# Half expert blocks summed by a product with a unit matrix, down weights split on VectorE alone, block columns fetched three blocks ahead

## The chip, the core and the metric

The kernel runs on one core of a Trainium2 chip, as one launch. The metric is the device time in microseconds (us). A core has TensorE (PE, with its weight loads PEld), VectorE (DVE), ScalarE (ACT), GpSimd (POOL) and SyncE (SP); SBUF is the on-chip memory, and PSUM, in eight banks of 2 KB per partition, takes TensorE's results. GpSimd doesn't reach PSUM.

## What is computed

Two transformer layers follow each other on 256 tokens of 1024 features in fp32. The first has three kinds of attention with a gated merge; the second has a mixer (short convolution and an attention over selected keys) and a mixture of experts. The change touches the last alone:

```
scores = sigmoid(t @ w_router); eidx = top 8 of scores + bias        # 64 experts, 256 tokens
g = scores at eidx, normalised, times 2.5
for each expert e, in blocks of its tokens xb:
    routed[tokens] += ((silu(xb @ w1[e]) * (xb @ w3[e])) @ w2[e]) * g
x = x + gate2 * (routed + shared expert)
```

w1[e] and w3[e] are 1024 x 256, w2[e] is 256 x 1024, all fp32. TensorE multiplies in a faster fp32 form that rounds its inputs, so each operand is split into a rounded high part and the rest (low part), and products of high by high, high by low and low by high are added up.

## The kernel before

Everything ahead of the experts (some 650 us) follows a written-out schedule and isn't touched. Then the router's choice is turned into a list of blocks, `work`: the pieces of experts' token lists, large ones (up to 128 tokens) in even places and small ones (up to 64) in odd places. With these inputs 33 blocks are run, numbered i = 0 to 32; `r = i % 4` picks buffers. An even block I call **whole**, an odd one **half**, an even and the next odd one a pair. All engines run loops over the blocks, in an order written by hand, and meet only by semaphores.

- SyncE loads, three transfers of 1 MB per block, w1 and w3 (`load_up`, L748, once the low parts of the block two before are made) and w2 (`load_down`, L755), then a column of 8 numbers per token for block i + 2 (`load_columns`, L741). `load_down` of an even block waits for GpSimd too, by the semaphore `pool_lo`.
- ScalarE makes the high parts: `up_hi` (four pieces, L1191) and `down_hi` (two, L1196) of the weights, and those of the turned rows (L1180, L1186), of the hidden values (`round_hidden`, L1202) and of the results (L1211).
- VectorE makes the low parts, a subtraction of the raw tile and the high part each: `up_lo` (L1736), `down_lo` (L1743), `x_block_lo` (L1730, in half blocks' rows L1723), `h_lo` (L1782; L1800 in half blocks), `y_lo` (L1750). `take_tokens` (L1716 to L1718) reads out which tokens block i + 2 has.
- GpSimd: in half blocks one piece of `up_lo` of the next block (`rest_of_up_weights`, L940), in whole blocks one piece of `down_lo` (`rest_of_down_weights`, L933). For both kinds: `pick` (`make_pick`, two L914) for block i + 3 out of its columns, `put` (`make_put`, L947), the matrix that scatters block i's results and that waits for the scatter of the block before, and the gather of block i + 2's rows from HBM (`gather_rows`, L925). In half blocks `put` comes before the gather, in whole blocks behind it.
- TensorE per block (`expert_block`): which tokens (`find_tokens`, L2158), up products into the bank `hidden_b` (L2206: 24 in a whole block, 16 in a half block), turning of the next block's gathered rows (`turn_rows`, L2168 for 64 rows, L2175 for 128), scatter of the last block's results (L2183, eight), two turns of the hidden values into `turned_b` (L2226), down products (L2245: 12 or 8).

In a half block, high and low part of the up to 64 rows lie side by side as the 128 columns of one stationary operand. The upper and lower half of `hidden_b` are therefore two parts of one sum. ScalarE copies the lower half (L1249), VectorE adds the upper (L1793), ScalarE takes silu (L1252), VectorE multiplies (L1797), TensorE turns the product (L2226), ScalarE rounds it (L1202), VectorE takes the rest (L1800):

```
act.activation(hsum[0:HALF, :], hidden_b[HALF:P, :], ACT.Copy)              # L1249
dve.tensor_tensor(hsum[0:HALF, :], hidden_b[0:HALF, :], hsum[0:HALF, :], ALU.add)   # L1793
act.activation(hs[0:HALF, 0, :], hsum[0:HALF, 0:ED], ACT.Silu)              # L1252
dve.tensor_tensor(he[0:HALF], hs[0:HALF, 0, :], hsum[0:HALF, ED:2 * ED], ALU.mult)  # L1797
```

## Time and profile before

| what | value |
|---|---|
| median of 3 runs (lowest, highest) | 1045.25 us (1044.28, 1047.04) |
| the profiled execution, its time and its span | 1048.44 us, 1046.6 us |
| mean granted clock of TensorE | 0.984 |
| TensorE, VectorE, ScalarE, GpSimd busy | 971.1, 755.3, 584.4, 408.4 us |
| the same as shares of the span | 93%, 72%, 56%, 39% |
| moved by DMA, mean rate | 238.55 MB, 228 GB/s |

Times in the trace count from the start of the span; its time is 1.84 us longer than its span. L numbers are lines of the kernel before. A row such as "675.78 0.77 PE L2245 ... [6.67 <-POOL down_lo L933]" says: start, length, engine, line, and that the engine had stood for 6.67 us, ended by GpSimd's write of `down_lo` at L933. The length of a TensorE record holds its way through the array; how fast products follow each other is read from their starts. "issue" in a chain is time in which the engine waited for nothing that the profile shows.

### The profile page before, as it was taken

How to read it: one execution, taken by the hardware profiler on the slowest of the kernel's cores; microseconds unless marked ns; L12 is line 12 of the kernel's file. 1: busy time of each engine (PE TensorE's matmuls, PEld its weight loads, DVE VectorE, ACT ScalarE, POOL GpSimd, SP SyncE). 2: the span in 40 equal slices, each digit the busy share in tenths (PEclk: the TensorE clock that was granted, in tenths of full speed). 3: DMA queues.
4: the chain of work that ended last, by engine and by line, in shares of the span. 5: the costliest groups of instructions: out<-in, count | busy, mean ns of one | idle time of the engine just before them, and what ended most of it. 6: DMA issues, size and time to landing. Idle time of an engine off the chain costs nothing. (4 is left out here: it accounts for less than half of the span.)

```text
span 1046.6 us, 16235 instructions
## 1 busy us (share of the span) xinstructions
PE 971.1 (93%) x4988; PEld 771.8 (74%) x4988; DVE 755.3 (72%) x1319; ACT 584.4 (56%) x896; POOL 408.4 (39%) x392
## 2 busy tenths in 40 slices
PE   8999999999999899999969999699899999999996
PEld 7778877778776676777758877477677777777774
DVE  4677888769753453556795554588898888888987
ACT  4555655444433432435433531487787887787875
POOL 5154453124100000041234411456666657666564
PEclk9999999999999899999998999899999999999998
DMA  9877677668635234425423223878888888888883
GB/s 312 280 258 264 222 240 274 224 203 283 228 101 181 96 101 181 161 82 183 143 99 137 86 88 141 292 275 330 311 304 328 339 303 338 310 303 338 316 327 134
DMA packets 79286, 238.55 MB, mean 228 GB/s; under 512 B 12732, under 2 KB 18933, under 8 KB 65922
## 3 DMA queue, kind: packets, MB, share of 16 engines
q1 hardware_dynamic: 66002, 196.60, 52.2%
q0 software_dynamic: 12656, 40.87, 11.5%
q8 instruction: 29, 0.48, 0.2%
q10 hardware_dynamic: 576, 0.41, 0.1%
q14 instruction: 23, 0.19, 0.1%
HBM read 235.55 MB, written 2.16 MB: 227 GB/s over the span
## 5 line engine op out<-in xcount | busy, mean ns | idle before, releaser
L1925 PE MATMUL bank<-w_hi,a_hi 128*128 128x512 f32 (+2 forms) x512 | 206.0, 402 | 10.0 <-DVE w_lo L1341 4.5
L1925 PE MATMUL bank<-w_hi,a_lo 128*128 128x512 f32 (+2 forms) x512 | 196.8, 384 | 0.0
L1925 PE MATMUL bank<-w_lo,a_hi 128*128 128x512 f32 (+2 forms) x512 | 196.5, 384 | 0.0
L1341 DVE TENSOR_TENSOR w_lo<-ring,w_hi 128x1024 fp32r<-128x1024 f32 (+2 forms) x132 | 152.8, 1181 | 52.6 <-ACT w_hi L1026 48.6
L1026 ACT ACTIVATE w_hi<-ring 128x1024 fp32r<-128x1024 f32 (+2 forms) x140 | 141.0, 1023 | 73.9 <-PE bank L1925 70.2
L1736 DVE TENSOR_TENSOR up_lo<-raw_weights,up_hi 128x1024 fp32r<-128x1024 f32 x120 | 144.4, 1239 | 2.9 <-ACT up_hi L1191 2.0
L1191 ACT ACTIVATE up_hi<-raw_weights 128x1024 fp32r<-128x1024 f32 x136 | 135.8, 1051 | 2.2 <-DMA raw_weights<-in_w_dram 2.2
L1925 PEld LDWEIGHTS bank<-w_hi,a_hi 128*128 128x128 f32 x512 | 96.5, 188 | 39.7 <-issue 18.0
L811 POOL TENSOR_SCALAR mean_squares<-mean_squares 128x8 f32<-128x8 f32 (+2 forms) x32 | 10.4, 324 | 283.6 <-ACT logits L979 203.5
L1925 PEld LDWEIGHTS bank<-w_hi,a_lo 128*128 128x128 f32 x512 | 96.5, 188 | 20.0
L1925 PEld LDWEIGHTS bank<-w_lo,a_hi 128*128 128x128 f32 x512 | 96.7, 189 | 18.3 <-issue 1.4
L2206 PE MATMUL bank<-up_hi,x_block_hi 128*128 128x512 f32 x264 | 107.2, 406 | 0.7 <-DVE x_block_lo L1730 0.7
L2206 PE MATMUL bank<-up_lo,x_block_hi 128*128 128x512 f32 x264 | 104.2, 395 | 0.0
L831 POOL DMA_DIRECT2D merged<-in_w_ada_dram x96 | 53.2, 556 | 127.2 <-DVE ada_acc L1480 93.9
L2245 PE MATMUL bank<-down_hi,h_hi 128*128 128x512 f32 x132 | 54.8, 415 | 24.1 <-DVE h_hi L1800 14.9
L914 POOL TENSOR_SCALAR pick<-slots,block_cols 128x128 fp32r<-128x128 f32 x72 | 51.2, 721 | 62.1 <-DMA block_cols<-pcol 60.6
L1196 ACT ACTIVATE down_hi<-raw_weights 128x1024 fp32r<-128x1024 f32 x68 | 69.8, 1055 | 0.2
L940 POOL TENSOR_TENSOR up_lo<-raw_weights,up_hi 128x1024 fp32r<-128x1024 f32 x16 | 43.9, 2741 | 63.2 <-ACT up_hi L1191 63.2
L1480 DVE SCALAR_TENSOR_TENSOR ada_acc<-merged,c_col,ada_acc 128x512 f32<-128x512 f32 x84 | 62.8, 747 | 5.1 <-DMA merged<-in_w_ada_dram 2.0
L947 POOL TENSOR_SCALAR put<-slots,block_tokens_f 128x256 fp32r<-128x256 f32 x33 | 59.7, 1810 | 14.8 <-PE bank L2183 14.8
L1743 DVE TENSOR_TENSOR down_lo<-raw_weights,down_hi 128x1024 fp32r<-128x1024 f32 x50 | 59.6, 1219 | 0.2 <-ACT down_hi L1196 0.2
L925 POOL DMA_INDIRECT x_gathered<-h_rows,block_tokens x35 | 51.4, 1469 | 20.8 <-issue 14.7
(283 smaller groups left out, 1968.4 us busy)
## 6 DMA issues: line engine op xcount, KB each, us to landing
raw_weights<-in_w_dram SPq DMA_DIRECT2D x102, 1024.0 KB, 6.9
ring<-in_w_in_dram SPq DMA_DIRECT2D x58, 1024.0 KB, 6.0
merged<-in_w_ada_dram POOLq DMA_DIRECT2D x96, 256.0 KB, 4.3
ring<-in_w_out_dram SPq DMA_DIRECT2D x8, 1024.0 KB, 6.0
ring<-in_w_branch_dram SPq DMA_DIRECT2D x6, 1024.0 KB, 4.9
bias<-rel_rows SPq DMA_DIRECT2D x40, 128.0 KB, 5.1
ring<-in_ws_dram SPq DMA_DIRECT2D x2, 1024.0 KB, 5.5
merged<-in_x_dram SPq DMA_DIRECT2D x2, 512.0 KB, 5.1
```

What stands on the lines that cost most here:

```text
L831: gp.dma_start(ada_row(q), src).then_inc(S(f"ada_loaded_{q % ADA_SLOTS}"), 16)
L947: gp.tensor_scalar(put[:, :], slots[:, S_TOK:S_TOK + TOK], tok_f[:, r, 0:1], None, ALU.is_equal)\
L1026: act.activation(w_parts[0][:, 2 * p:2 * p + 2, 0:w], view(j, kind)[:, 2 * p:2 * p + 2, :], ACT.Copy)\
L1191: act.activation(up_hi[:, r % 2, 4 * kh:4 * kh + 4, m, :], raw_up(raw[:, 1 - r % 2, :], kh, m), ACT.Copy)\
L1196: act.activation(down_hi[:, f, :], raw[:, 1 - r % 2][:, UP + f * DM:UP + (f + 1) * DM], ACT.Copy)\
L1341: dve.tensor_tensor(w_parts[1][:, 2 * p:2 * p + 2, 0:w], view(JOB[it[1:3]], kind)[:, 2 * p:2 * p + 2, :], w_parts[0][:, 2 * p:2 * p + 2, 0 ...
L1480: dve.scalar_tensor_tensor(out=o, in0=ada_row(q), scalar=c_col[:, 1, k:k + 1], in1=o, op0=ALU.mult, op1=ALU.add) .then_inc(S("ada_step" if ...
L1736: dve.tensor_tensor(up_lo[:, r % 2, 4 * kh:4 * kh + 4, m, :], raw_up(raw[:, 1 - r % 2, :], kh, m), up_hi[:, r % 2, 4 * kh:4 * kh + 4, m, : ...
L1743: dve.tensor_tensor(down_lo[:, f, :], raw[:, 1 - r % 2][:, UP + f * DM:UP + (f + 1) * DM], down_hi[:, f, :].bitcast(F32), ALU.subtract).th ...
L1925: mm = pe.matmul(ps[:, 0:wide], a_parts[za][:, k, t * P:(t + 1) * P], w_parts[zw][:, k, 0:wide], start=start, stop=stop)
L2206: mm = pe.matmul(hidden_b[:, :], (xe_hi, xe_lo)[zx][:, k, :], (up_hi, up_lo)[zw][:, r % 2, k].rearrange("p m n -> p (m n)"), start=(k == 0 ...
L2245: mm = pe.matmul(y_b[hf][:, :], (h_hi, h_lo)[zh][:, f, :], (down_hi, down_lo)[zw][:, f, hf * CH:hf * CH + CH], start=(n == 0), stop=(n == ...
```

## The change

Three things, all in the expert loop.

1. In half blocks ScalarE copies the whole of `hidden_b` to `halves`. Four products with `S_PAIR`, 64 columns that have a one at row j and at row j + 64, add the two halves and turn them at once into `turned_b`. TensorE waits for them (for `tokens_ready` too, since the found tokens lie in the same bank), ahead of the scatter. Silu, product and both parts are then taken in the turned form; the two turns of L2226 go in half blocks.
2. GpSimd's `rest_of_down_weights` goes; VectorE makes both pieces of `down_lo` in whole blocks. The waits on `pool_lo` shrink to those for `up_lo`, and SyncE's `load_down` waits for VectorE alone.
3. Columns are loaded three blocks ahead, two blocks' columns at the start.

The order of instructions on three engines moves with it. TensorE in a half block, from the turning of the next rows to the down products, before:

```order
L2175 MATMUL bank<-consts,x_gathered 128x128 x8
L2183 MATMUL bank<-y_hi,put 128x512
L2183 MATMUL bank<-y_lo,put 128x512
L2183 MATMUL bank<-y_hi,put 128x512
L2183 MATMUL bank<-y_lo,put 128x512
L2183 MATMUL bank<-y_hi,put 128x512
L2183 MATMUL bank<-y_lo,put 128x512
L2183 MATMUL bank<-y_hi,put 128x512
L2183 MATMUL bank<-y_lo,put 128x512
L2220 REGISTER_ALU
L2226 MATMUL bank<-consts,hT 128x64 x2
L2231 ISA
```

and now (line numbers of the changed kernel):

```order
L2163 MATMUL bank<-consts,x_gathered 128x128 x8
L2204 REGISTER_ALU
L2210 MATMUL bank<-slots,halves 128x64 x4
L2171 MATMUL bank<-y_hi,put 128x512
L2171 MATMUL bank<-y_lo,put 128x512
L2171 MATMUL bank<-y_hi,put 128x512
L2171 MATMUL bank<-y_lo,put 128x512
L2171 MATMUL bank<-y_hi,put 128x512
L2171 MATMUL bank<-y_lo,put 128x512
L2171 MATMUL bank<-y_hi,put 128x512
L2171 MATMUL bank<-y_lo,put 128x512
L2226 REGISTER_ALU
```

The four products stand ahead of the scatter, where two turns stood behind it. VectorE in a half block, before:

```order
L1743 TENSOR_TENSOR down_lo<-raw_weights,down_hi 128x1024
L1792 ISA
L1793 TENSOR_TENSOR hidden_sum<-bank,hidden_sum 64x512
L1715 REGISTER_ALU
L1716 CAST block_tokens<-bank 128x1
L1717 TENSOR_REDUCE block_gates<-bank 128x1
L1718 COPY block_tokens_f<-bank 128x1
L1796 REGISTER_ALU
L1797 TENSOR_TENSOR hT<-hs,hidden_sum 64x256
L1728 ISA
L1730 TENSOR_TENSOR x_block_lo<-bank,x_block_hi 128x512
L1800 TENSOR_TENSOR h_hi<-bank,h_hi 128x2x64
```

and now:

```order
L1733 TENSOR_TENSOR down_lo<-raw_weights,down_hi 128x1024
L1705 REGISTER_ALU
L1706 CAST block_tokens<-bank 128x1
L1707 TENSOR_REDUCE block_gates<-bank 128x1
L1708 COPY block_tokens_f<-bank 128x1
L1784 REGISTER_ALU
L1785 TENSOR_TENSOR hT<-hs,bank 128x128
L1718 ISA
L1720 TENSOR_TENSOR x_block_lo<-bank,x_block_hi 128x512
L1788 TENSOR_TENSOR h_hi<-hT,h_hi 128x2x64
L1720 TENSOR_TENSOR x_block_lo<-bank,x_block_hi 128x512
L1725 ISA
```

The sum is gone, the product is 128 columns and reads PSUM. GpSimd in a whole block and the half block behind it, before:

```order
L914 TENSOR_SCALAR pick<-slots,block_cols 128x128 x2
L920 REGISTER_ALU
L922 ISA
L925 DMA x_gathered<-h_rows,block_tokens 128x1024
L931 ISA
L933 TENSOR_TENSOR down_lo<-raw_weights,down_hi 128x1024
L945 REGISTER_ALU
L947 TENSOR_SCALAR put<-slots,block_tokens_f 128x256
```

and now, with the half block:

```order
L910 TENSOR_SCALAR pick<-slots,block_cols 128x128 x2
L916 REGISTER_ALU
L918 ISA
L921 DMA x_gathered<-h_rows,block_tokens 128x1024
L934 REGISTER_ALU
L936 TENSOR_SCALAR put<-slots,block_tokens_f 128x256
L948 UNCONDITIONAL_BRANCH
L948 REGISTER_ALU
L948 COMPARE_AND_BRANCH
L927 ISA
L929 TENSOR_TENSOR up_lo<-raw_weights,up_hi 128x4x256
```

The subtraction between gather and `put` is gone; the half block's order (`up_lo`, two picks, `put`, gather) stays.

The diff:

```diff
@@ -56,7 +56,7 @@
 
 C_ID, C_CAUS, C_FREQ, C_TRI, C_IOTA, C_THR_ROW = 0, 128, 384, 392, 520, 648
 C_COL, C_PLACE, C_EXP, C_THR, C_N = 776, 777, 778, 779, 780
-S_TOK, S_HALF, S_N = 0, 256, 384
+S_TOK, S_HALF, S_PAIR, S_N = 0, 256, 384, 448
 FAR = 1000.0
 
 
@@ -487,7 +487,7 @@
         xg = sb("x_gathered", [P, 2, DM], F32, operands)
         hs = sb("hs", [P, FT, TOK], F32, operands)
         hT = sb("hT", [P, FT, TOK], F32, operands)
-        hsum = sb("hidden_sum", [P, 2 * ED], F32, operands)
+        halves = sb("halves", [P, 2 * ED], F32, operands)
         slots = sb("slots", [P, S_N], F32, operands)
         sb("rows_end", [P, BODY * TOK - 2 * ED - S_N], F32, operands)
         col4 = sb("block_cols", [P, BODY, NCOL], F32R, operands)
@@ -757,7 +757,8 @@
             load_down(0, load_up(0, 0))
             n_work = sp.value_load(work[0:1, 0:1], min_val=0, max_val=MAX_WORK)
             sp.wait_ge(S("token_columns"), NT + 1)
-            load_columns(2, 2)
+            for r in range(2, BODY):
+                load_columns(r, r)
             for r in range(1, BODY):
                 with sp.If(n_work > r - 1):
                     if r == 1:
@@ -769,11 +770,9 @@
 
                         sp.wait_ge(S("up_lo"), {2: 4, 3: 8}[r])
                         e = load_up(r, r)
-                        sp.wait_ge(S("down_lo"), {2: 1, 3: 3}[r])
-                        if r == 2:
-                            sp.wait_ge(S("pool_lo"), 1)
+                        sp.wait_ge(S("down_lo"), 2 * (r - 1))
                     load_down(r, e)
-                    load_columns(r + 2, (r + 2) % BODY)
+                    load_columns(r + 3, (r + 3) % BODY)
             with sp.Fori(1, -(-(MAX_WORK + 1) // BODY)) as m:
                 for r in range(BODY):
                     i = m * BODY + r
@@ -782,15 +781,12 @@
                         sp.wait_ge(S("up_lo"), 14 * m + {0: -3, 1: 1, 2: 4, 3: 8}[r])
                         sp.sem_inc(S("begun"), 1)
                         if r % 2 == 0:
-                            sp.wait_ge(S("pool_lo"), i - 2)
+                            sp.wait_ge(S("pool_lo"), 2 * m + r // 2 - 1)
                             sp.sem_inc(S("begun"), 1)
                         e = load_up(i, r)
-                        sp.wait_ge(S("down_lo"), 6 * m + {0: -2, 1: 0, 2: 1, 3: 3}[r])
-                        if r % 2 == 0:
-                            sp.sem_inc(S("begun"), 1)
-                            sp.wait_ge(S("pool_lo"), i - 1)
+                        sp.wait_ge(S("down_lo"), 2 * i - 2)
                         load_down(r, e)
-                        load_columns(i + 2, (r + 2) % BODY)
+                        load_columns(i + 3, (r + 3) % BODY)
             for hf in range(2):
                 c = slice(hf * CH, hf * CH + CH)
                 for t in range(NT):
@@ -926,13 +922,6 @@
                                       in_offset=bass.IndirectOffsetOnAxis(ap=tok[0:rows, r, 0:1], axis=0))\
                   .then_inc(S(f"rows_gathered_{r}"), 16)
 
-            def rest_of_down_weights(i, r):
-
-                gp.wait_ge(S("down_hi"), 2 * i + 2)
-                gp.sem_inc(S("begun"), 1)
-                gp.tensor_tensor(down_lo[:, 1, :], raw[:, 1 - r % 2][:, UP + DM:UP + 2 * DM], down_hi[:, 1, :].bitcast(F32),
-                                 ALU.subtract).then_inc(S("pool_lo"), 1)
-
             def rest_of_up_weights(i, r):
 
                 gp.wait_ge(S("up_hi"), 4 * i + 1)
@@ -964,7 +953,6 @@
                             make_put(i, r)
                         gather_rows(i + 2, (r + 2) % BODY, m4 * (BODY // 2) + (r + 2) // 2)
                         if not r % 2:
-                            rest_of_down_weights(i, r)
                             make_put(i, r)
 
         @block.scalar
@@ -1196,10 +1184,10 @@
                 act.activation(down_hi[:, f, :], raw[:, 1 - r % 2][:, UP + f * DM:UP + (f + 1) * DM], ACT.Copy)\
                    .then_inc(S("down_hi"), 1)
 
-            def round_hidden(i, rows):
-
-                act.wait_ge(S("h_turned"), i + 1)
-                act.activation(h_hi[:, :, 0:rows], turned_b[:, 0:FT * rows].rearrange("p (f n) -> p f n", f=FT), ACT.Copy)\
+            def round_hidden(pair):
+
+                act.wait_ge(S("h_turned"), pair + 1)
+                act.activation(h_hi[:, :, :], turned_b[:, 0:FT * P].rearrange("p (f n) -> p f n", f=FT), ACT.Copy)\
                    .then_inc(S("h_hi_ready"), 1)
 
             def round_y(i, r):
@@ -1235,7 +1223,7 @@
                             act.wait_ge(S("up_done"), i + 1)
                             act.activation(hs[:, 0, :], hidden_b[:, 0:ED], ACT.Silu).then_inc(S("silu_done"), 1)
                             round_half_rows(pair)
-                            round_hidden(i, P)
+                            round_hidden(pair)
                             for m in range(2):
                                 round_up_weights(nxt, 1, m)
                             round_y(i, r)
@@ -1246,12 +1234,14 @@
                             act.wait_ge(S(f"up_loaded_{nxt}"), 32 * nxt_loads)
                             round_up_weights(nxt, 0, 0)
                             act.wait_ge(S("up_done"), i + 1)
-                            act.activation(hsum[0:HALF, :], hidden_b[HALF:P, :], ACT.Copy).then_inc(S("half_low_copied"), 1)
+                            act.activation(halves[:, :], hidden_b[:, :], ACT.Copy).then_inc(S("halves_copied"), 1)
                             round_whole_rows(pair + 1, 0)
                             act.wait_ge(S("half_summed"), pair + 1)
-                            act.activation(hs[0:HALF, 0, :], hsum[0:HALF, 0:ED], ACT.Silu).then_inc(S("silu_done"), 1)
+                            act.activation(hs[:, 0, 0:P], turned_b[:, 0:P], ACT.Silu).then_inc(S("silu_done"), 1)
                             round_whole_rows(pair + 1, 1)
-                            round_hidden(i, HALF)
+                            act.wait_ge(S("h_done"), i + 1)
+                            act.activation(h_hi[:, :, 0:HALF], he[:, 0:P].rearrange("p (f n) -> p f n", f=FT), ACT.Copy)\
+                               .then_inc(S("h_hi_ready"), 1)
                             round_up_weights(nxt, 0, 1)
                             for m in range(2):
                                 round_up_weights(nxt, 1, m)
@@ -1773,7 +1763,8 @@
                 half = r % 2
                 if not half:
                     take_tokens(i + 2, (r + 2) % BODY, found_b)
-                    rest_of_down_weights(i, r, 0)
+                    for f in range(FT):
+                        rest_of_down_weights(i, r, f)
                     rest_of_up_weights(i + 1, nxt, 0, 0)
                     dve.wait_ge(S("silu_done"), i + 1)
                     dve.tensor_tensor(he, hs[:, 0, :], hidden_b[:, ED:2 * ED], ALU.mult).then_inc(S("h_done"), 1)
@@ -1789,15 +1780,12 @@
                     rest_of_down_weights(i + 1, nxt, 0)
                     return
                 rest_of_down_weights(i, r, 1)
-                dve.wait_ge(S("half_low_copied"), pair(0) + 1)
-                dve.tensor_tensor(hsum[0:HALF, :], hidden_b[0:HALF, :], hsum[0:HALF, :], ALU.add)\
-                   .then_inc(S("half_summed"), 1)
                 take_tokens(i + 2, (r + 2) % BODY, found_b)
                 dve.wait_ge(S("silu_done"), i + 1)
-                dve.tensor_tensor(he[0:HALF], hs[0:HALF, 0, :], hsum[0:HALF, ED:2 * ED], ALU.mult).then_inc(S("h_done"), 1)
+                dve.tensor_tensor(he[:, 0:P], hs[:, 0, 0:P], turned_b[:, P:2 * P], ALU.mult).then_inc(S("h_done"), 1)
                 rest_of_whole_rows(pair(1), 0)
                 dve.wait_ge(S("h_hi_ready"), i + 1)
-                dve.tensor_tensor(h_hi[:, :, HALF:P], turned_b[:, 0:FT * HALF].rearrange("p (f n) -> p f n", f=FT),
+                dve.tensor_tensor(h_hi[:, :, HALF:P], he[:, 0:P].rearrange("p (f n) -> p f n", f=FT),
                                   h_hi[:, :, 0:HALF].bitcast(F32), ALU.subtract).then_inc(S("h_lo_ready"), 1)
                 rest_of_whole_rows(pair(1), 1)
                 for kh, m in PIECES_OF_UP[1:]:
@@ -2200,7 +2188,7 @@
                             pe.wait_ge(S(f"x_lo_ready_{k // 4}"), pair(0) + 1)
                         pe.wait_ge(S("up_lo"), 7 * pair(0) + (6 if half else 2) + k // 2)
                     if k == 0 and not half and not (isinstance(i, int) and i == 0):
-                        pe.wait_ge(S("pool_lo"), i)
+                        pe.wait_ge(S("pool_lo"), pair(0))
                     passes = PASSES[0:2] if half else PASSES
                     for n, (zx, zw) in enumerate(passes):
                         mm = pe.matmul(hidden_b[:, :], (xe_hi, xe_lo)[zx][:, k, :],
@@ -2212,25 +2200,31 @@
                     for hf in range(2):
                         pe.wait_ge(S(f"y_lo_{hf}"), i)
                 turn_rows(nxt, nxt_loads)
+                if half:
+                    pe.wait_ge(S("tokens_ready"), i + 3)
+                    pe.sem_inc(S("begun"), 1)
+                    pe.wait_ge(S("halves_copied"), pair(0) + 1)
+                    for m in range(2):
+                        for f in range(FT):
+                            c = (m * FT + f) * HALF
+                            mm = pe.matmul(turned_b[:, c:c + HALF], halves[:, m * ED + f:(m + 1) * ED:FT],
+                                           slots[:, S_PAIR:S_PAIR + HALF], start=True, stop=True)
+                    mm.then_inc(S("half_summed"), 1)
                 if not first:
                     pe.wait_ge(S("put_ready"), i)
                     scatter(0, i)
                     if half:
                         scatter(1, i).then_inc(S("block_done"), 1)
-                pe.wait_ge(S("h_done"), i + 1)
-                rows = HALF if half else P
-                if half:
-                    pe.sem_inc(S("begun"), 1)
-                for f in range(FT):
-
-                    mm = pe.transpose(turned_b[:, f * rows:(f + 1) * rows], he[0:rows, f:ED:FT], consts[0:rows, C_ID:C_ID + rows])
-                mm.then_inc(S("h_turned"), 1)
+                if not half:
+                    pe.wait_ge(S("h_done"), i + 1)
+                    for f in range(FT):
+
+                        mm = pe.transpose(turned_b[:, f * P:(f + 1) * P], he[:, f:ED:FT], ident)
+                    mm.then_inc(S("h_turned"), 1)
                 if not first and not half:
                     scatter(1, i).then_inc(S("block_done"), 1)
                 pe.wait_ge(S("h_hi_ready"), i + 1)
-                pe.wait_ge(S("down_lo"), 3 * pair(0) + (3 if half else 1))
-                if not half:
-                    pe.wait_ge(S("pool_lo"), i + 1)
+                pe.wait_ge(S("down_lo"), 2 * i + 2)
                 if half:
                     pe.wait_ge(S("h_lo_ready"), i + 1)
                 for hf in range(2):
@@ -2301,6 +2295,7 @@
     slots = np.zeros((P, S_N), np.float32)
     slots[:, S_TOK:S_TOK + TOK] = np.arange(TOK)[None, :]
     slots[:, S_HALF:S_HALF + P] = np.arange(P)[None, :] % HALF
+    slots[:, S_PAIR:S_PAIR + HALF] = np.arange(P)[:, None] % HALF == np.arange(HALF)[None, :]
     sq[:, C_THR_ROW:C_THR_ROW + NV] = P * (np.arange(NV)[None, :] // N_EXP) - FAR
     sq[:, C_COL] = np.arange(P)
     sq[:, C_PLACE] = np.arange(P) - NV
```

## Rows read from the trace of the kernel before

**Rows 1.** Who waited for whom from 640 us on: us in total, times, longest.
```profile
PE bank L2245 <- POOL down_lo L933: 9.3, 3, 6.7
```

**Rows 2.** The chain of waits through one pair of blocks: start us, us, what.
```profile
903.61 3.84 PE bank L2206 x16
...
908.10 0.70 DVE hidden_sum L1793
...
909.27 1.01 DVE hT L1797
910.28 0.14 issue
...
910.87 0.29 ACT h_hi L1202
911.18 0.30 DVE h_hi L1800
911.49 0.28 issue
...
925.53 3.84 PE bank L2206 x16
```

**Rows 3.** Timeline of block 0, TensorE and VectorE: start us, us, engine, line, operation.
```profile
675.78 0.77 PE L2245 MATMUL bank<-down_hi,h_hi 128*128 128x512 f32 x1 [6.67 <-POOL down_lo L933]
...
681.17 0.48 PE L2206 MATMUL bank<-up_hi,x_block_hi 128*128 128x512 f32 x1
...
668.97 0.69 DVE L1723 TENSOR_TENSOR x_block_hi<-bank,x_block_hi 128x512 fp32r<-128x512 f32 x1 [0.43 <-ACT x_block_hi L1180]
```

**Rows 4.** Stretches: PE, PEld, DVE, ACT, POOL busy us, granted clock, DMA share, GB/s.
```profile
675.00:680.00 5.00, 4.22 (x10) 3.38 (x11) 0.50 (x1) 0.69 (x1) 1.43 (x2) 0.50 0.79 278
...
880.00:940.00 60.00, 55.51 (x266) 43.95 (x265) 53.61 (x78) 48.31 (x66) 39.41 (x28) 1.00 0.83 308
```

**Rows 5.** Timeline of a half block, TensorE, VectorE and GpSimd.
```profile
908.06 0.48 PE L2183 MATMUL bank<-y_hi,put 128*128 128x512 f32 x1
...
909.78 0.40 PE L2183 MATMUL bank<-y_lo,put 128*128 128x512 f32 x1
...
911.30 0.92 POOL L947 TENSOR_SCALAR put<-slots,block_tokens_f 128x256 fp32r<-128x256 f32 x1
911.39 0.68 DVE L1730 TENSOR_TENSOR x_block_lo<-bank,x_block_hi 128x512 fp32r<-128x512 f32 x1
...
912.13 1.23 DVE L1736 TENSOR_TENSOR up_lo<-raw_weights,up_hi 128x1024 fp32r<-128x1024 f32 x1
912.38 1.82 POOL L925 DMA_INDIRECT x_gathered<-h_rows,block_tokens  x1 [0.15 <-issue]
```

**Rows 6.** Line L2098, 620 to 623 us: duration ns min/median/max, first and last start.
```profile
L2098 PE MATMUL bank<-w_router,xT x16: 222/275/275, 620.7 to 622.3; 128*128 128x64 f32 x16
```

**Rows 7.** Timeline of the whole block behind it, TensorE, GpSimd and VectorE.
```profile
919.62 0.71 PE L2168 MATMUL bank<-consts,x_gathered 64*128 64x64 f32 x8
...
922.23 0.40 PE L2183 MATMUL bank<-y_lo,put 128*128 128x512 f32 x1
...
918.14 1.25 POOL L925 DMA_INDIRECT x_gathered<-h_rows,block_tokens  x1 [0.47 <-issue]
...
922.84 2.72 POOL L947 TENSOR_SCALAR put<-slots,block_tokens_f 128x256 fp32r<-128x256 f32 x1 [0.96 <-PE bank L2183]
...
922.48 2.35 DVE L1736 TENSOR_TENSOR up_lo<-raw_weights,up_hi 128x1024 fp32r<-128x1024 f32 x2
```

**Rows 8.** Landing of the gathers at 912.38 and 918.14; queue q0 (gathers), 922.5 to 925.
```profile
DMA to landing us min/median/max: 4.7/4.7/4.7
...
DMA to landing us min/median/max: 7.3/7.3/7.3
...
q0 software_dynamic: 144, 0.52, 51.2%
```

**Rows 9.** SyncE's issues, 896 to 924 us: the up weights after L1736.
```profile
916.69 0.82 SPq L748 DMA_DIRECT2D raw_weights<-in_w_dram  x2
```


## The prediction

> **What bounds the kernel now.** The page of the profile says TensorE: busy 93% of the span. The change lives in the expert loop, 33 blocks in pairs of a whole block (even) and a half block (odd), from about 661 us to the end. Next I read who waits for whom from 640 us on. TensorE waits 9.3 us in 3 pieces for GpSimd's part of the down weights (L933) [rows 1]. Third, the chain of waits through one ordinary pair: the up products of a half block start at 903.61, those of the next at 925.53, so a pair takes 21.92 us. After the up products the chain leaves TensorE: ScalarE's copy, VectorE's sum (0.70) and product (1.01), two turns, two roundings (0.29, 0.30), and the first down product at 911.77 [rows 2]. Fourth, block 0: its first down product comes at 675.78 after 6.67 us of standing, ended by L933 [rows 3], and the granted clock is 0.50 of full speed there (1.2 of 2.4 GHz) [rows 4]. Last, VectorE is nearly as full as TensorE, 53.61 of 60 us [rows 4]. So TensorE bounds the loop, with one hole in each half block, and VectorE is close behind.
>
> **Part 1: down weights off GpSimd, columns earlier.** In block 0 the next late thing is VectorE's L1723, 668.97 to 669.66 [rows 3]; the subtraction that moves to VectorE (1.22 us) lies before it, where the weights come later than VectorE. With 0.14 us from VectorE to TensorE [rows 2] the down products start at 669.8: 6.0 us won. Since TensorE stands under 1 us then, I let the clock stay at full speed; 675.78 to 681.17 [rows 3] is 5.39 us for twelve products, and at full speed one comes each 0.233 us (eight scatter products start between 908.06 and 909.78, the first 0.09 slower [rows 5]), so 2.8, with the token product 3.0: 2.4 more. **8.4 us.** The two other waits on L933 go as well, 9.3 - 6.67 = **2.6 us** [rows 1]. If they came back elsewhere (a late column is what the chain shows before one of them), that would cost up to 2.6. SyncE's column loads change their place by one block, not their number; its weight loads land 4 us before their use and cover the half microsecond that each takes to issue.
>
> **Part 2: sums by products.** VectorE per pair: the sum goes (0.70), the product of 1.01 becomes one of 128x128 from PSUM (0.29, as L1800), one subtraction comes (1.22): -0.2 us. TensorE gets four fp32 products of 128x128 weights and 64 columns. The nearest row has that very shape, L2098: 16 records for 8 products, starting from 620.7 to 622.3, so 0.108 us for each record, 0.275 long [rows 6]. Four products are eight records: 0.87 us. Bounds: 0.43, if each were one record, to 1.0.
>
> The new half block in the clock of [rows 2, 5]: the copy ends at 908.06 (before the sum at 908.10). The products start 0.15 later, 908.21, are issued by 909.08 and done by 909.25. Silu 909.28 to 909.56 (as L1202); VectorE's product to 909.88, its L1730 (0.68, next start 0.07 before the end) to 910.49, its rounding to 910.71, and 0.28 to TensorE: 910.99. TensorE itself does the eight scatter products, which ended 1.98 us after 908.06, now after 909.08: 911.06. Both roads meet at 911.1, where it was 911.77. **0.66 us in each of 16 half blocks: 10.6 us** (16 with 0.43 us of products, 8 with 1.0).
>
> So far 8.4 + 2.6 + 10.6 = 21.6 us. The profiled execution took 1048.44 us around its span of 1046.6, 3.2 above the median of 1045.25; the saving is the same against either, and off the median it gives 1023.6.
>
> **Part 3: what the earlier chain runs into.** In a half block GpSimd makes `put` (L947, 0.92 us at 911.30), and only behind it issues the gather of the next half block's rows (L925, 912.38) [rows 5]; that lands after 4.7 us, 917.1 [rows 8], and TensorE turns the rows at 919.62 [rows 7]. But the `put` of the whole block, 0.36 us behind the first of two L1736 in a row, takes 2.72 us and ends 0.73 after the second [rows 7]. So `put` stands still while VectorE goes from one such subtraction to the next. The Trainium skill says the like (GPSIMD Engine Reference, Specifications: GpSimd shares its SBUF interfaces with VectorE, contended when VectorE has two SBUF inputs); the trace agrees, 2.72 us against 0.92.
>
> Now `put` misses this: VectorE's three L1736 begin at 912.13, when it is nearly done [rows 5]. In the changed kernel VectorE's second L1730 ends at 911.32 and ScalarE's piece for L1736 is there at 911.2, so the three begin at 911.25. `put` waits for the last scatter product, 910.80 + 0.40 = 911.20, and comes 0.21 later (as 922.23 + 0.40 and 922.84 show [rows 7]): 911.41. VectorE is first by 0.16 us. `put` then stands for three subtractions (1.15 us each), ends at 915.5, and the gather is issued at 915.65, 3.3 us later than now. TensorE wants the rows at 918.9 (0.66 earlier than now, and weights first). Landing after 4.7 us is 1.4 us too late.
>
> It may land later still. SyncE issues 2 MB of up weights 1.06 us after the third subtraction, now at 916.69 [rows 9], then at 915.8, beside the gather. The whole block's gather (918.14, 128 rows of 4 KB, 0.52 MB) went behind such a load: all 0.52 MB of its queue q0 moved after 922.5, and it landed after 7.3 us [rows 8]. A gather that falls between the two 1 MB loads starts when the first is through, half of 922.5 - 916.69 and 0.7 for its start: 919.4. The whole gather took 2.9 us from 922.5 to its landing at 925.4; with half of the rows this one takes 1.5: 920.9, **2.0 us late, 16 times: 32 us**. Bounds: 0.9 late, if the loads don't touch it (issued in 1.25 us like the whole one, landed 2.9 after that, as today: 919.8), to 4.2, behind both loads (through at 921.6, landed 923.1). I take the middle case, since both are issued within 0.2 us. 1023.6 + 32 = **1055.6 us**.
>
> The Trainium skill speaks for a shorter landing (DMA: Bandwidth & Descriptors, Issuing engines are not separate DMA queues: transfers of all issuers share 16 engines and "interleave with each other"). By the row above, the gather did not get its share until the load was through. It is rival (b).
>
> **The rivals.**
> (a) *`put` comes first.* The margin of 0.16 us is built from a dozen durations; a silu 0.15 longer turns it round. The gather then stays where it is, and VectorE stands 0.1 to 0.3 us per pair, 0 to 0.27 of which may show: 1023.6 to 1028. Chance 0.24.
> (b) *Packets interleave.* The gather lands at 919.8, 0.9 late, 14 us in all: 1038; with 0.5 us less for its shorter way, 1030. Chance 0.15.
> (c) *Behind both loads:* 4.2 late, 67 us, 1091. Chance 0.15.
> (d) *VectorE becomes the bound.* Its work is 53.61 / 60 x 21.92 = 19.6 us per pair, then 19.4, and its waits 2.3. Three of these, 1.0 in all, give way to one of 1.6 for the products. If no wait overlaps another's cause, a pair takes 22.3, 0.4 more than now: 1045.25 - 11.0 + 6 = 1040. Against it: the waits come from TensorE's progress, which is earlier too. Chance 0.04.
> (e) *Block 0 gains nothing*, because something else holds it: 8.4 us on top of any case, 0.02.
>
> What decides the sign is the gather's lateness: 21.6 / 16 = 1.35 us is break-even. Below lie (a), (b) and (d), which end faster.
>
> **The numbers.** Within 0.3% (3.1 us) is about what a measurement of this kernel can't tell from no change. The forecast, lateness 1.1 to 3.5 us: 0.42, of which 0.08 lies within 0.3% and 0.34 above; alone it gives 1041 to 1080. Faster: (a), (b) all but 0.03, (d): 0.40. Slower: 0.34, (c) and part of (e): 0.50. Same: 0.10. The range over all cases leaves out (c)'s end and (a)'s: 1022 to 1086.
>
> **What would show it.** Right: `put` of half blocks 3.5 to 4.2 us long; the half gather issued 8.4 us after the last up product instead of 5.1; TensorE standing before the 64-row turns of whole blocks, 16 times, ended by the gather's DMA; no wait on a GpSimd down subtraction; clock 1.00 at 675 us of the span; the first down product of a half block 3.8 us after the last up product, not 4.5. Wrong: `put` of 0.92 there and pairs of 21.3 us (a), or a stretched `put` with rows landing within 4.2 us of their issue (b).

## The result, and the profile after

The changed kernel takes **1028.27 us** (median of 4 runs, 1026.48 to 1030.57) against 1045.57 us for the kernel before (4 runs, 1044.28 to 1047.04): ratio 0.9825, 95% interval 0.9802 to 0.9848. It is 17.3 us faster. The forecast was 1055.6 us, slower than before. All times here and below are medians of executions that lie within 1% of each other; one of the four of "part 1 alone" took 2952.73 us and is left out.

| | before | after |
|---|---|---|
| span of the profiled execution | 1046.6 us | 1026.8 us |
| first up product of block 0 | 661.81 | 660.37 |
| from there to the first up product of block 1 | 19.36 | 11.00 |
| 15 pairs behind it, 30 of 33 blocks | 331.91 | 322.56 |
| the pair that nothing late lengthens | 21.92 | 21.17 |
| from the first up product of block 31 to the end | 33.53 | 32.92 |

The differences, 1.44 + 8.36 + 9.35 + 0.61, make the 19.8 us between the spans. (The 1.44 us lie ahead of the loop; the kernels below start it between 657.2 and 662.9, so I count them for nothing.) A pair here is a half block and the whole block behind it. Before, 21.92 us was the usual one; now the 15 take 21.17 to 22.29 us, and most are longer than 21.17.

Block 0 went as forecast. TensorE's timeline, then the stretches of the changed kernel (columns as in [rows 4]):

```profile
668.37 0.47 PE L2239 MATMUL bank<-down_hi,h_hi 128*128 128x512 f32 x1 [0.71 <-DVE x_block_hi L1713]
...
671.37 0.48 PE L2194 MATMUL bank<-up_hi,x_block_hi 128*128 128x512 f32 x1
```

```profile
670.00:675.00 5.00, 5.00 (x25) 4.07 (x24) 4.99 (x6) 4.22 (x5) 0.00 (x0) 1.00 0.66 233
675.00:680.00 5.00, 5.00 (x31) 4.16 (x30) 3.32 (x9) 3.87 (x8) 4.66 (x4) 1.00 0.94 392
...
880.00:940.00 60.00, 59.82 (x303) 48.33 (x302) 53.51 (x78) 48.50 (x68) 43.96 (x25) 1.00 0.88 343
```

The 6.67 us of [rows 3] are 0.71 now, and the clock is 1.00 where [rows 4] have 0.50. From 880 to 940 us TensorE is busy for 59.82 of 60 us, where it was 55.51.

Now a half block and the whole block behind it, all engines, in order of time. All of it is 4.58 us later than in [rows 5]: its up products start at 908.05, there at 903.47:

```profile
912.73 1.13 PE L2210 MATMUL bank<-slots,halves 128*128 128x64 f32 x8
...
913.90 0.28 ACT L1240 ACTIVATE hs<-bank 128x128 f32<-128x128 f32 x1 [0.76 <-PE bank L2210]
...
914.21 0.29 DVE L1785 TENSOR_TENSOR hT<-hs,bank 128x128 f32<-128x128 f32 x1 [1.69 <-ACT hs L1240]
...
915.62 0.49 PE L2239 MATMUL bank<-down_hi,h_hi 128*128 128x512 f32 x1
...
915.84 3.70 DVE L1726 TENSOR_TENSOR up_lo<-raw_weights,up_hi 128x1024 fp32r<-128x1024 f32 x3
...
915.98 2.93 POOL L936 TENSOR_SCALAR put<-slots,block_tokens_f 128x256 fp32r<-128x256 f32 x1 [0.19 <-PE bank L2171]
919.08 1.31 POOL L921 DMA_INDIRECT x_gathered<-h_rows,block_tokens  x1 [0.16 <-issue]
...
920.72 0.82 SPq L748 DMA_DIRECT2D raw_weights<-in_w_dram  x2
...
923.67 0.68 PE L2156 MATMUL bank<-consts,x_gathered 64*128 64x64 f32 x8
```

The down products start 7.57 us after the first up product; before it was 8.30. In the kernel before TensorE waited for them in each half block, in the view of [rows 1]:

```profile
PE bank L2245 <- DVE h_hi L1800: 14.9, 16, 1.0
```

That wait is gone. `put` (L936) starts 0.14 us behind the first of VectorE's three subtractions (L1726) and takes 2.93 us. The gather (L921) comes behind it, 1.64 us ahead of SyncE's up weights. The landing of this gather, as in [rows 8], and TensorE's waits from 640 us on, as in [rows 1]:

```profile
DMA to landing us min/median/max: 4.5/4.5/4.5
```

```profile
PE bank L2156 <- DMA x_gathered<-h_rows,block_tokens: 4.1, 7, 1.1
```

Waits on GpSimd's subtraction are gone. The rows are late in 7 pairs, by 1.1 us at most. Over the half blocks the landing takes 4.1 to 5.4 us, though the gather is issued at the same place in each, 1.5 to 1.6 us ahead of the loads; why it differs isn't shown.

### The profile page after: what moved, and what is told of

The parts are those of the page before. It is cut to its first block and busy times, and to the rows that moved or that the text cites. A ratio compares the mean times of both kernels' runs of the same rounds, so it can differ in the third digit from the quotient of the medians.

```text
span 1026.8 us, 16388 instructions
## 1 busy us (share of the span) xinstructions
PE 974.3 (95%) x5084; PEld 780.2 (76%) x5084; DVE 749.7 (73%) x1320; ACT 579.5 (56%) x896; POOL 422.1 (41%) x375
## 5 line engine op out<-in xcount | busy, mean ns | idle before, releaser
L1726 DVE TENSOR_TENSOR up_lo<-raw_weights,up_hi 128x1024 fp32r<-128x1024 f32 x120 | 146.3, 1255 | 0.0
L1913 PEld LDWEIGHTS bank<-w_hi,a_lo 128*128 128x128 f32 x512 | 96.2, 188 | 19.8
L936 POOL TENSOR_SCALAR put<-slots,block_tokens_f 128x256 fp32r<-128x256 f32 x33 | 91.4, 2769 | 31.0 <-PE bank L2171 31.0
L910 POOL TENSOR_SCALAR pick<-slots,block_cols 128x128 fp32r<-128x128 f32 x72 | 76.3, 1072 | 23.2 <-DMA block_cols<-pcol 22.5
L1733 DVE TENSOR_TENSOR down_lo<-raw_weights,down_hi 128x1024 fp32r<-128x1024 f32 x67 | 79.5, 1226 | 0.0
L2194 PEld LDWEIGHTS bank<-up_lo,x_block_hi 128*128 128x128 f32 x264 | 49.8, 188 | 10.4
L2194 PEld LDWEIGHTS bank<-up_hi,x_block_hi 128*128 128x128 f32 x264 | 49.7, 188 | 10.4
```

The lines of the kernel that those rows point to most:

```text
L910: gp.tensor_scalar(pick[:, r % 2, t, :], slots[:, at:at + P], col4[:, r, 4 * t + 3:4 * t + 4].bitcast(F32), None, ALU.is_equal)\
L936: gp.tensor_scalar(put[:, :], slots[:, S_TOK:S_TOK + TOK], tok_f[:, r, 0:1], None, ALU.is_equal)\
L1726: dve.tensor_tensor(up_lo[:, r % 2, 4 * kh:4 * kh + 4, m, :], raw_up(raw[:, 1 - r % 2, :], kh, m), up_hi[:, r % 2, 4 * kh:4 * kh + 4, m, : ...
L1733: dve.tensor_tensor(down_lo[:, f, :], raw[:, 1 - r % 2][:, UP + f * DM:UP + (f + 1) * DM], down_hi[:, f, :].bitcast(F32), ALU.subtract).th ...
L1913: mm = pe.matmul(ps[:, 0:wide], a_parts[za][:, k, t * P:(t + 1) * P], w_parts[zw][:, k, 0:wide], start=start, stop=stop)
L2194: mm = pe.matmul(hidden_b[:, :], (xe_hi, xe_lo)[zx][:, k, :], (up_hi, up_lo)[zw][:, r % 2, k].rearrange("p m n -> p (m n)"), start=(k == 0 ...
```

## Experiments

### What the half block's gather costs

**Gather first.** In half blocks GpSimd issues the gather ahead of `put`, as it does in whole blocks.

```diff
-                        if r % 2:
-                            make_put(i, r)
                         gather_rows(i + 2, (r + 2) % BODY, m4 * (BODY // 2) + (r + 2) // 2)
-                        if not r % 2:
-                            make_put(i, r)
+                        make_put(i, r)
```

> The changed kernel with GpSimd's order in half blocks turned round: the gather of the next half block's rows first, put behind it. Theory A (what is left of the forecast's mechanism: put, stretched to 2.93 us, holds back the gather behind it, and TensorE stands for the rows 4.1 us in 7 pieces): the gather is issued about 3 us earlier in the pair (some 4.1 us after the last up product, not 7.2), all waits before the 64-row turns go, every pair takes 21.2 us, and put, done 2 to 3 us later, has nobody waiting for it: 4.1 us less than the changed kernel, 1024.2 us. Rival B (the rows land when the queues are free, whenever they are issued): the gather's packets stay behind the 1 MB load that runs until some 1 us after the gather's present issue, the landing moves by under 0.5 us, the waits stay over 2.5 us: 1027 to 1028. Rival C: put or the picks come too late for TensorE's scatter or tokens: new waits on GpSimd, 1030 or more.

Measured: 1024.02 us (5 runs), ratio to the kernel before 0.9791 (0.9777 to 0.9805). GpSimd in one half block:

```profile
848.71 1.97 POOL L921 DMA_INDIRECT x_gathered<-h_rows,block_tokens  x1 [0.15 <-PE bank L2168]
850.70 2.12 POOL L936 TENSOR_SCALAR put<-slots,block_tokens_f 128x256 fp32r<-128x256 f32 x1
```

TensorE waits for no gather any more in this trace, and all 15 pairs take 21.16 to 21.21 us. That is A; that the time comes within 0.2 us of its number is luck, since the executions spread over 1.5 us. The gather is issued 3.1 us earlier in the pair, but it lands 5.4 to 6.5 us after its issue, so it comes only some 2 us earlier; that suffices. To see whether the gain is real, I timed the changed kernel again.

> The changed kernel once more, for a ratio to the kernel before on this chip beside the gather-first version (0.979, 0.9777 to 0.9805). From the two traces (4.1 us of waits for rows more, in one of them): 0.983, within 0.981 to 0.985. If the gather-first version gained nothing: 0.979.

It gave 1027.39 us (5 runs), ratio 0.9807 (0.9785 to 0.9829). That is just outside my 0.981 to 0.985, nearly as far from 0.983 as from 0.979, and its interval overlaps the other one: the times alone don't show a gain. The traces, two of the changed kernel and one with the gather first, do: this second profile too has pairs of up to 22.45 us, and from the first up product of block 1 to that of block 32 it takes 331.03 us (332.20 in the first profile), with the gather first 327.48. So the waits for rows are there in both profiles of the changed kernel, and worth 3.5 to 4.7 us.

**The forecast's situation.** The forecast had the gather issued 0.15 us ahead of the loads. In the first kernel `put` waits for the third subtraction, in the second only the gather does.

```diff
                         if r % 2:
+                            gp.wait_ge(S("up_lo"), 14 * m4 + {1: 11, 3: 18}[r])
                             make_put(i, r)
```

```diff
                             make_put(i, r)
+                            gp.wait_ge(S("up_lo"), 14 * m4 + {1: 11, 3: 18}[r])
                         gather_rows(i + 2, (r + 2) % BODY, m4 * (BODY // 2) + (r + 2) // 2)
```

> The changed kernel, but in half blocks GpSimd's put waits until VectorE has made all three subtractions of up weights. That makes the situation on which the forecast of 1055.6 was built: the gather is issued some 1.5 us later than in the changed kernel, within 0.2 us of SyncE's 2 MB of up weights. Theory A (the forecast's price was right, its moment was not): the gather's packets wait for the first of the two loads, TensorE gets the rows 5.2 us or more after their issue, about 2.3 us late in each pair: 1028.3 - 4.1 + 37 = 1061. Rival B (packets of the gather go beside the load as today: first 2.0 us after issue, last 3.4 to 4.5, TensorE 1.1 later): 1.6 us late on average, 1050. Rival C (behind both loads): over 4 us late, 1090 or more. put itself should take 0.9 us in A, B and C, since VectorE then reads PSUM.

> The changed kernel, but in half blocks the gather waits for VectorE's third subtraction of up weights; put stays where it is. The gather is then issued some 0.5 to 0.7 us later than in the changed kernel and 1.0 us ahead of SyncE's 2 MB of up weights (1.5 to 1.6 in the changed kernel; within 0.3 us where put waited too, and there the rows came 8.6 us after their issue). Theory A (what counts is whether the first packets of the gather, 2.0 us behind its issue, come before those of the load): they still do, the rows come as quickly as before, only 0.6 us later: 16 x 0.6 = 10 us, some 1037. Rival B (the lead of 1.0 us is too short, the gather falls behind a load as a whole): 3 us or more per pair: 1075 to 1145.

Measured: **1143.85 us**, ratio 1.0946 (1.0916 to 1.0976), and **1136.64 us**, ratio 1.0874 (1.0856 to 1.0892). The first time lies in C's range, but the gather doesn't land behind both loads; it is A's picture at nearly three times A's price (83.4 us of waits in 16 pieces), and `put` takes 0.92 us there, as all three said. The second time is B's. My expectation of a lead of 1.0 us in it was wrong. GpSimd, SyncE and TensorE there:

```profile
882.68 0.97 POOL L921 DMA_INDIRECT x_gathered<-h_rows,block_tokens  x1 [1.58 <-DVE up_lo L1727]
...
882.90 0.82 SPq L748 DMA_DIRECT2D raw_weights<-in_w_dram  x2
...
890.91 1.09 PE L2157 MATMUL bank<-consts,x_gathered 64*128 64x64 f32 x8 [5.15 <-DMA x_gathered<-h_rows,block_tokens]
```

SyncE waits for the same subtraction, so the lead is 0.1 to 0.2 us in every pair: the place that the forecast described, except that gather and loads both come about 0.3 us later behind the first subtraction than it said. What the queues moved there, first from 883.5 to 887, then from 887 to 890 us, and the landing:

```profile
q1 hardware_dynamic: 125, 1.02, 87.0%
```

```profile
q1 hardware_dynamic: 87, 0.58, 73.4%
q0 software_dynamic: 75, 0.26, 30.2%
```

```profile
DMA to landing us min/median/max: 8.1/8.1/8.1
```

Of the gather (q0) nothing moves until the first 1 MB is through. From then on it shares the engines with the second load, and takes 2.7 us for its 0.26 MB. It lands after 8.1 us, 3.8 us after its first packet. TensorE stands 5.15 us here, 79.7 us in 16 pieces in all, and works at a clock of 0.50 behind it:

```profile
891.00:895.00 4.00, 4.00 (x16) 3.28 (x17) 0.82 (x2) 1.14 (x3) 0.00 (x0) 0.50 1.00 410
```

The same kernel has its own control. Behind the last half block no weights are loaded any more. There the gather is issued at the same place, its first packet moves after 1.7 us, and TensorE stands 0.94 us; the landing:

```profile
DMA to landing us min/median/max: 3.9/3.9/3.9
```

In the other 15 it stands 4.7 to 6.1 us. So most of the price is the load beside the gather, and not the later issue by itself. Together, 1.4 us of later issue (4.65 us behind the start of the first subtraction, 3.24 in the changed kernel) cost 7.2 us per pair (28.7 against 21.5). Leads between 0.2 and 1.5 us were not tried.

### How long put stands behind VectorE

**A gap.** VectorE makes the second `x_block_lo` (L1720) behind the first of its three subtractions.

```diff
-                rest_of_whole_rows(pair(1), 1)
-                for kh, m in PIECES_OF_UP[1:]:
+                for n, (kh, m) in enumerate(PIECES_OF_UP[1:]):
                     rest_of_up_weights(i + 1, nxt, kh, m)
+                    if n == 0:
+                        rest_of_whole_rows(pair(1), 1)
```

> The changed kernel, but VectorE makes the second low part of the turned rows (which reads PSUM and one SBUF operand) between the first and the second of its three subtractions of up weights in a half block. Theory A (GpSimd's put can't get at SBUF while VectorE goes from one subtraction with two SBUF operands to the next, and gets in where another operation stands between): put begins 0.1 to 0.2 us after the first subtraction, gets through when that ends, and takes 1.7 to 2.0 us, not 2.93; the gather is issued 1 us earlier, the waits for the rows fall from 4.1 to under 1 us: about 1025, if VectorE's 0.6 us of standing (its piece from ScalarE comes later than it) costs nothing. Rival B (put is slow for another reason, and ends where it did): put 2.9 us, no gain, and VectorE 0.6 us per pair later: 1028 to 1032.

Measured: 1044.14 us (10 runs), ratio 0.9981 (0.997 to 0.9992), where A said 1025 and B up to 1032. VectorE, GpSimd, TensorE:

```profile
879.28 1.22 DVE L1726 TENSOR_TENSOR up_lo<-raw_weights,up_hi 128x1024 fp32r<-128x1024 f32 x1 [0.52 <-ACT up_hi L1179]
880.42 0.68 DVE L1720 TENSOR_TENSOR x_block_lo<-bank,x_block_hi 128x512 fp32r<-128x512 f32 x1
...
879.42 1.87 POOL L936 TENSOR_SCALAR put<-slots,block_tokens_f 128x256 fp32r<-128x256 f32 x1 [0.19 <-PE bank L2172]
...
881.16 0.50 PE L2240 MATMUL bank<-down_hi,h_hi 128*128 128x512 f32 x1 [0.92 <-DVE x_block_lo L1720]
```

`put` is through 0.79 us after the end of the one subtraction, as A said, and no 64-row turn waits. The time was lost elsewhere: the down products write the bank that this L1720 still has to read, so TensorE waits for it, 14.9 us in 16 pieces by that view, and a hole of 1.3 us each by the starts of the products. Neither theory had this; it came with my edit, and says nothing about the change. The run counts for the length of `put` alone.

**Shorter subtractions.** In half blocks each of the three is made in two instructions of half the size.

```diff
+                w = 4 // parts
+                for p in range(parts):
+                    k = slice(4 * kh + w * p, 4 * kh + w * (p + 1))
+                    sub = dve.tensor_tensor(up_lo[:, r % 2, k, m, :], raw_up(raw[:, 1 - r % 2, :], kh, m)[:, w * p:w * (p + 1), :],
+                                            up_hi[:, r % 2, k, m, :].bitcast(F32), ALU.subtract)
+                sub.then_inc(S("up_lo"), 1)
...
-                    rest_of_up_weights(i + 1, nxt, kh, m)
+                    rest_of_up_weights(i + 1, nxt, kh, m, 2)
```

> The changed kernel, but in half blocks VectorE makes each of its three subtractions of up weights in two instructions of half the size; one look at how long put takes behind the first. Theory A (GpSimd waits for a number of VectorE's instructions: two, as in the changed kernel's 2.93 us with three in a row): put gets in after two short ones, 1.3 us, and takes 1.9 to 2.2 us. Rival B (it waits a time, some 2 us, whatever the instructions are): 2.7 to 3.0 us. Rival C (it gets in only at gaps between VectorE's instructions that the scheduler of the kernel left): over 3.5 us. Pairs may be longer by some tenths of a us, since six instructions take longer than three.

Measured in one execution: `put` 1.86 us, and 1024.44 us, with no wait for rows. Its GpSimd, and the last three of VectorE's six short ones:

```profile
912.90 1.86 POOL L936 TENSOR_SCALAR put<-slots,block_tokens_f 128x256 fp32r<-128x256 f32 x1 [0.19 <-PE bank L2174]
914.92 1.39 POOL L921 DMA_INDIRECT x_gathered<-h_rows,block_tokens  x1 [0.16 <-PE bank L2149]
...
914.78 1.88 DVE L1729 TENSOR_TENSOR up_lo<-raw_weights,up_hi 128x512 fp32r<-128x512 f32 x3
```

A short one starts 0.6 us behind the one before. `put` starts 0.14 us behind the first, is let in when the second ends, 1.15 us later, and needs 0.71 more. With long ones it is 2.22 and 0.71, which is the 2.93 of the changed kernel. So it is not a fixed time, and not the end of the run either, which has six instructions here; what fits all these runs is the end of the second instruction. It is one execution, but the same in each of the 16 half blocks. This is A, though `put` is a little shorter than its 1.9 to 2.2 us.

### The parts alone

"Part 1 alone" is the kernel before with the new sums only, and so on. Their diffs are those hunks of the change; where part 2 is left out, TensorE keeps its two old waits ahead of the down products. Part 3 is two edits:

```diff
-            load_columns(2, 2)
+            for r in range(2, BODY):
+                load_columns(r, r)
...
-                        load_columns(i + 2, (r + 2) % BODY)
+                        load_columns(i + 3, (r + 3) % BODY)
```

| kernel | us | ratio to before (95%) | block 0 | usual pair |
|---|---|---|---|---|
| part 1 alone | 1052.72 | 1.0058 (1.0035 to 1.0081) | 19.5 | 22.44 |
| part 2 alone | 1036.39 | 0.9901 (0.9884 to 0.9917) | 11.0 | 21.93 |
| part 3 alone | 1038.68 | 0.9917 (0.9885 to 0.9949) | 14.4 | 21.93 |
| 2 and 3 | 1036.51 | 0.99 (0.9884 to 0.9917) | 11.0 | 21.93 |
| 1 and 2 | 1030.52 | 0.9869 (0.9842 to 0.9895) | 11.0 | 21.2, rows late in some |
| 1 and 3 | 1041.16 | 0.9952 (0.993 to 0.9974) | 13.1 | 22.42 in 9 of 15, 21.9 |
| all | 1028.27 | 0.9825 (0.9802 to 0.9848) | 11.0 | 21.17, rows late in some |

> Part 2 alone: VectorE makes both low parts of the down weights; columns two ahead. If late columns had no share in the other two waits on L933 (2.6 us): as with part 3, 1034.4. If the late column of these two pairs holds something else up once the subtraction is gone, 1 to 2.6 us come back as a wait on GpSimd's picks or on the gather: 1035.5 to 1037.

> The kernel before with parts 2 and 3 and without part 1: VectorE makes both low parts of the down weights, columns are fetched three ahead, half blocks are summed by VectorE as before. By the forecast's terms 8.4 us in block 0 (clock 1.00 there) and 2.6 us of the other waits on GpSimd: 1045.4 - 11.0 = 1034.4. Rival B (VectorE's 1.22 us more per pair isn't hidden while it still makes the sum, 0.70, and the long product, 1.01): pairs of 22.2 us or more in place of 21.92, 1039 or more.

> Part 3 alone: columns three blocks ahead, nothing else. Block 0 stays as it was (6.7 us of standing at low clock). If late columns are what makes the two waits on L933 in the middle (2.6 us), these go: 1042.8. If columns are hidden anyway: 1045.4, no difference beyond 0.3%.

> The changed kernel with columns two blocks ahead again (parts 1 and 2 without part 3). Theory A (taking the subtraction off GpSimd is what both the sums and block 0 need; with it gone the columns come in time): within 2 us of the changed kernel, 1028 to 1030. Rival B (GpSimd, whose put and gather come later than before, now also stands for late columns in its picks): the picks and the gather of whole blocks come later, pairs of 21.6 us or more, 1034 or more.

Each ratio is to executions of the kernel before that were taken with it. Part 2 alone has all of block 0 and both other waits on L933, and part 3 adds nothing to it that can be measured (1036.39 and 1036.51); of its own 2.6 us it gives 0.4 back in one pair of 22.33 us. Part 3 alone was worth more than either of my numbers: all pairs are even, and block 0 is 4.9 us shorter, since GpSimd no longer stands 7.5 us for a column there before its pick. 1 and 2 is 2.3 us from all three, with overlapping intervals: A, just past its 2 us. In the traces the 15 pairs take 322.67 us with 1 and 2 and 322.56 with all three, so beside the other two part 3 adds nothing that these runs show. Rival B of "2 and 3", that the 1.22 us more on VectorE would show, is dead: 21.93 against 21.92 us.

Part 1 alone surprised: slower than before.

> The kernel before with part 1 alone: half blocks summed by products with S_PAIR, columns two ahead, GpSimd still makes its half of the down weights' low part in whole blocks. By the forecast's terms: 10.6 us of the half blocks' shorter chain come, 6.7 us of block 0 stay with their low clock, and the waits on GpSimd's L933 (2.6 us elsewhere) stay or grow: 1045.4 - 10.6 = 1034.8, less what the late gather costs (up to 4). Theory A (GpSimd's queue holds it back: picks and gathers of the whole block wait behind put and the subtraction): waits on GpSimd grow by some us, 1036 to 1045. Rival B: the parts are independent, 1034 to 1036.

It is A, and at 1052.72 us beyond its range of 1036 to 1045. TensorE's waits from 640 us on, and GpSimd from a half block's `put` to the whole block's subtraction:

```profile
PE bank L2252 <- POOL down_lo L933: 16.7, 15, 6.7
PE bank L2167 <- DMA x_gathered<-h_rows,block_tokens: 5.6, 8, 1.0
```

```profile
912.61 2.93 POOL L947 TENSOR_SCALAR put<-slots,block_tokens_f 128x256 fp32r<-128x256 f32 x1 [0.20 <-PE bank L2182]
915.70 1.31 POOL L925 DMA_INDIRECT x_gathered<-h_rows,block_tokens  x1 [0.16 <-issue]
917.26 3.15 POOL L914 TENSOR_SCALAR pick<-slots,block_cols 128x128 fp32r<-128x128 f32 x2 [0.24 <-issue]
920.57 1.02 POOL L925 DMA_INDIRECT x_gathered<-h_rows,block_tokens  x1 [0.17 <-issue]
921.62 2.40 POOL L933 TENSOR_TENSOR down_lo<-raw_weights,down_hi 128x1024 fp32r<-128x1024 f32 x1
```

In [rows 5] `put` took 0.92 us in this place; its 2 us more push the subtraction of the whole block back, for which TensorE waits (L2252). Is it the queue? I shortened `put` there with the split subtractions.

> The kernel before with part 1 alone (1053.5 us, pairs of 22.44 us, put of the half block 2.93 us), and VectorE's three subtractions of up weights in half blocks each made in two instructions of half the size, behind which put took 1.86 us. Theory A (in part 1 alone GpSimd's queue sets the pair: put, gather, picks, gather, subtraction of down weights, one behind the other, with TensorE at its end): put 1.07 us shorter, the subtraction of down weights ends 1 us earlier in the pair, the waits on it (10.1 us in 14 pieces) mostly go, pairs of 21.4 to 21.6 us: 1053.5 - 14 = 1039 or less. Rival B (late columns or the gather's landing set the pair): pairs stay over 22 us, 1048 or more.

`put` fell to 1.86 us, and nothing was won: 1052.35 us, ratio 1.004 (1.0019 to 1.0061), pairs of 22.6 us, 0.2 more than without the split; where these 0.2 us come from isn't shown. Theory A fell. The chain of waits shows another loop:

```profile
904.90 0.07 DVEq L1812
905.00 0.26 DVE down_lo L1748
...
906.13 1.23 DVE down_lo L1748
907.38 0.33 SPq L755
...
908.52 6.81 DMA block_cols<-pcol
...
919.12 1.02 POOL x_gathered L925
920.17 2.40 POOL down_lo L933
922.56 0.09 issue
922.65 1.63 PE bank L2255 x6
```

VectorE's low part lets SyncE load down weights; the column goes behind them and lands 6.8 us later; pick, gather and GpSimd's subtraction follow, then TensorE, and its results bring VectorE round again. This loop has a column fetched two blocks ahead in it. The last two kernels open it, without and with the split.

> Parts 1 and 3 without part 2: sums by products, columns three ahead, GpSimd keeps its subtraction of down weights. Block 0 gains what part 3 alone gave it (4.9 us). Theory A (in part 1 alone the pair of 22.44 us is a loop through the column: VectorE's low part, SyncE's load of down weights, the column behind it, 6.8 us to its landing, pick, gather, GpSimd's subtraction, TensorE's down products): with the column fetched a block earlier the loop opens, pairs come down by 0.3 to 0.8 us, and the whole is 1035 to 1043. Rival B (GpSimd's own queue sets the pair: put of 2.93 us, gather, picks, gather, subtraction): pairs stay at 22.4, 1047 to 1049.

> The same with VectorE's three subtractions of up weights of half blocks in two instructions each, so that put is 1.07 us shorter. Theory A: the picks no longer wait for the column (18.5 us in 16 pieces in the version with columns two ahead), GpSimd's subtraction ends at least 1 us earlier in the pair, its waits go: pairs of 21.2 to 21.6 us, 1030 to 1036. Rival B: here GpSimd's queue is shorter by 1.07 us only, pairs of 22.4 become 21.4 at best; the same number, so that this run alone doesn't tell them apart, but if the run without the split stays at 22.4 and this one falls to 21.4, it is the queue.

Without the split: 1041.16 us, most pairs still 22.42, TensorE waiting 10.0 us for the subtraction from 690 us on. The time lies in A's range because of block 0; the pairs are B's. With it: **1024.94 us**, ratio 0.98 (0.9763 to 0.9837), pairs of 21.17 to 21.31 us and one wait on the subtraction left, in block 0. That is 5 us under my range: block 0 is 6.5 us shorter than before, not 4.9, and the pairs are at their shortest. So part 1 runs into two loops of nearly the same length, GpSimd's queue (22.4, read where the column comes early) and the late column (22.6, read where `put` is short). Either alone keeps the pair long, and one must open both. Part 2 does so by itself; so do part 3 and a shorter `put` together.

## Why the prediction was wrong

- **Part 1 of the forecast, 8.4 + 2.6 us: right.** Block 0 gave 8.36 us. The pairs with L933 had been 1.86 and 1.23 us longer than the rest, 3.1 in all for 2.6, and are gone.
- **Part 2, 0.66 us per half block: right, slightly small.** The products took 0.94 us by their starts for 0.87, VectorE needed 0.29 as taken, and the down products start 3.76 us behind the issue of the last up product (3.8 was said). A pair without late rows fell by 0.75 us.
- **The start of `put`: right.** Forecast 911.25 for VectorE and 911.41 for `put`; in that clock 911.26 and 911.40. VectorE was first, and `put` was stretched. So rival (a), whose time of 1023.6 to 1028 is nearest, came out by another road: its number is near by luck, its mechanism didn't happen. Rival (b)'s didn't either: in the pair shown the gather moved its 0.26 MB between 921.0 and 922.5 us, and the first packet of the loads came at 922.0.
- **The step that failed: "`put` then stands for three subtractions (1.15 us each), ends at 915.5".** It stood for two, took 2.93 us instead of the 3.5 to 4.2 named as a sign, and ended at 914.33. The row that I leaned on, [rows 7], has a run of only two, and can't tell "until the run ends" from "until the second ends". I took the first reading without marking it as a choice. The changed kernel itself shows that it isn't the run's end, since `put` is through 0.6 us before that; the split run shows the second. The gather was issued at 914.50 for 915.65, and SyncE's load at 916.14 for 915.8; so its lead was 1.64 us, not 0.15. It landed after 4.5 us in this pair, and the late rows cost 5.0 us (15 pairs of 322.56 us against 15 x 21.17), not 32. 21.6 - 5.0 = 16.6 us; 17.3 were measured.
- **The price was wrong too, the other way.** At the forecast's lead the rows are 4.7 to 6.1 us late, not 2.0, and beyond the bound of 4.2. The first load delays the gather as said, but its first packet comes 4.2 to 4.8 us after its issue, where the forecast had 3.75. Then it shares with the second load, and from first packet to landing it takes 3.8 us, where I scaled 1.5 from the whole block's gather: of its 0.52 MB, 0.36 moved between 923.5 and 924.5 us, while the loads moved 0.02. With the slow clock behind each stand, the kernel takes 1137 us, far outside my range. So had the first step been right, the forecast would have been some 80 us too low. One wrong step hid the other. The Trainium skill (DMA: Bandwidth & Descriptors, Issuing engines are not separate DMA queues) says that transfers of all issuers interleave; the 887 to 890 us of that run agree. The stretch before doesn't: without a load the first packet moves 1.7 us after the issue, here that is 884.3, and until 887 the gather moved none while the load moved on.
- **The sum treated the parts as independent**, and part 1 alone is 0.6% slower. No term of mine had this; GpSimd's subtraction was costed only where it already made TensorE wait. With part 2 in, this did no harm.

## What to carry to other kernels

Before a moved operation is costed as a sum of terms, follow each queue that it passes once round the loop: two loops within 0.2 us of each other hid behind the one that was removed, and a part that gains 0.7 us per pair with them open loses 0.5 with them shut. When a transfer is issued near a large one of another queue, its lead is what to read: in these runs 1.6 us ahead cost at most 1.2 us, 0.1 to 0.2 us ahead cost about 5, so keep small gathers well clear of weight loads, here by issuing the gather before `put`. And where a row shows only one length of a pattern, write down both readings and price both.
